# All expert-row gathers of the last stage asked for at once, into buffers that stay

## The reference, cut to what matters

```
ys = lax.map(expert_block, (xs, blk_e)).reshape(P, D)       # rows sorted by expert
out = jnp.zeros((T, D), h.dtype).at[slot_tok].add(ys * slot_w[:, None])
x = x + out
return rmsnorm(x, final_norm_g)
```

## Time and profile before

| | us |
|---|---|
| median of three runs | 2504.13 |
| the three runs | 2502.18 to 2509.46 |
| span of the profiled execution | 2504.9 |
| DVE busy in the span | 1248.2 |
| ACT busy | 1009.9 |
| POOL busy | 160.6 |

### The profile page before, as it was taken

One profiled execution on the slowest core, in us unless ns is written; L12 is line 12 of the kernel. 1 busy time (PEld: TensorE's weight loads), 2 busy tenths in 40 slices (PEclk: granted clock), 3 DMA queues, 4 the chain that ended last, 5 costly groups with the idle time before them and its releaser, 6 DMA issues. The chain is left out here.

```text
span 2504.9 us, 32948 instructions
## 1 busy us (share of the span) xinstructions
PE 2146.1 (86%) x11404; PEld 1831.7 (73%) x11405; DVE 1248.2 (50%) x1504; ACT 1009.9 (40%) x1406; POOL 160.6 (6%) x260
## 2 busy tenths in 40 slices
PE   7967999944998877999999449999999999999900
PEld 6855777734886866888888348888888888888800
DVE  3444655557011562333333455656866646656545
ACT  4543222113010453343333305645766646556421
POOL 0000000000000000000000000000000000000043
PEclk9987999967999898999999669999999999999955
DMA  3753111046343432222221335776987757757777
GB/s 110 234 207 126 51 59 43 31 165 227 124 136 131 152 118 81 74 76 79 81 75 51 146 127 203 306 271 252 386 333 278 293 217 288 302 207 298 305 277 276
DMA packets 121258, 450.54 MB, mean 180 GB/s; under 512 B 12784, under 2 KB 35824, under 8 KB 100720
## 3 DMA queue, kind: packets, MB, share of 16 engines
q1 hardware_dynamic: 76096, 296.58, 32.6%
q0 software_dynamic: 27600, 85.47, 10.1%
q10 hardware_dynamic: 17504, 67.71, 6.6%
HBM read 357.44 MB, written 92.28 MB: 180 GB/s over the span
## 5 line engine op out<-in xcount | busy, mean ns | idle before, releaser
L1795 DVE TENSOR_TENSOR expert_lo<-expert_raw,expert_hi 128x2048 fp32r<-128x2048 f32 x188 | 421.8, 2284 | 36.8 <-ACT expert_hi L1740 36.8
L1740 ACT ACTIVATE expert_hi<-expert_raw 128x2048 fp32r<-128x2048 f32 x186 | 346.0, 1912 | 17.0 <-ACT ex_y L1777 17.0
L61 PE MATMUL ex_pD<-expert_hi,ex_hT_lo 128*128 128x512 f32 x392 | 159.0, 406 | 0.0
L61 PE MATMUL ex_pG<-expert_hi,ex_xT_lo 128*128 128x512 f32 x392 | 155.9, 398 | 1.6 <-DVE ex_xT_lo L1800 1.6
L62 PE MATMUL ex_pG<-expert_lo,ex_xT_hi 128*128 128x512 f32 x392 | 155.6, 397 | 0.0
L63 PE MATMUL ex_pG<-expert_hi,ex_xT_hi 128*128 128x512 f32 x392 | 155.5, 397 | 0.0
L63 PE MATMUL ex_pD<-expert_hi,ex_hT_hi 128*128 128x512 f32 x392 | 155.3, 396 | 0.0
L62 PE MATMUL ex_pD<-expert_lo,ex_hT_hi 128*128 128x512 f32 x392 | 155.0, 395 | 0.0
L1814 DVE TENSOR_TENSOR ex_hm<-ex_sil,ex_pUa 128x256 f32<-128x256 f32 x49 | 20.6, 420 | 224.7 <-PE ex_pUa L63 223.1
L61 PE MATMUL ex_pUb<-expert_hi,ex_xT_lo 128*128 128x256 f32 x392 | 113.7, 290 | 0.0
L62 PE MATMUL ex_pUb<-expert_lo,ex_xT_hi 128*128 128x256 f32 x392 | 110.3, 281 | 0.0
(11 more groups left out here) (358 smaller groups left out, 5465.0 us busy)
## 6 DMA issues: line engine op xcount, KB each, us to landing
expert_raw<-in_w_gate SPq DMA_DIRECT2D x64, 1024.0 KB, 6.4
expert_raw<-in_w_up SPq DMA_DIRECT2D x64, 1024.0 KB, 8.9
expert_raw<-in_w_down SPq DMA_DIRECT2D x64, 1024.0 KB, 8.2
ys<-ex_y ACTq DMA_DIRECT2D x49, 512.0 KB, 8.4
z<-ff_z ACTq DMA_DIRECT2D x16, 1024.0 KB, 5.0
fb_z<-z SPq DMA_DIRECT2D x16, 1024.0 KB, 5.3
ff_xs<-in_x SPq DMA_DIRECT2D x16, 512.0 KB, 3.6
cv_xs<-in_x SPq DMA_DIRECT2D x16, 512.0 KB, 3.4
```

The source lines that it names most:

```text
L61: pe.matmul(out, lhsT=a_lo, rhs=b_hi, start=first, stop=False, skip_group_check=True)
L1740: act.activation(w_hi[:, c], raw[:, c], ACT.Copy).then_inc(s_hi, 1)
L1795: dve.tensor_tensor(w_lo[:, c], raw[:, c], w_hi[:, c], ALU.subtract).then_inc(s_lo, 1)
```

## The change

All 16 tiles get buffers of their own: `x2`, `ya` and `yb` become 128 x 16 x 1024, and every tile has its own semaphore for each of its three transfers (48 in place of 6). The sum is written over `x2`, the result over `yb`, and ACT's square over `ya`, so `acc`, `res` and `junk` are gone. POOL waits for nothing within the phase: it issues the 32 gathers one after another, with the column of `slot_of` as the index list, and `row` with its copies is gone. SP asks for the residual rows of three tiles at once, the gain behind the first, and from the fourth tile on waits for the pair sum of three tiles before (`s_y`). The order of DVE's work is add(t+1), scale(t) from the first tile on. All loops are written out.

```
-                if not is_first(t, 2):
-                    pool.wait_ge(s_acc, t - 1)
-                for k in range(2):
-                    last = pool.tensor_copy(row[:, u, k:k + 1], slot_of[:, bass.ds(t + k * NT, 1)])
-                last.then_inc(s_row, 1)
-                pool.wait_ge(s_row, t + 1)
-                pool.sem_inc(s_asked, 1)
+            for t in range(NT):
                 for k, (dst, done) in enumerate(((ya, s_a), (yb, s_b))):
-                    pool.indirect_dma_start(out=dst[:, u], out_offset=None, in_=scratch["ys"][0:NBLK * P],
+                    pool.indirect_dma_start(out=dst[:, t], out_offset=None, in_=scratch["ys"][0:NBLK * P],
                                             in_offset=bass.IndirectOffsetOnAxis(
-                                                ap=row[:, u, k:k + 1].bitcast(U32), axis=0)
-                                            ).then_inc(done[u], 16)
+                                                ap=slot_of[:, t + k * NT:t + k * NT + 1].bitcast(U32), axis=0)
+                                            ).then_inc(done[t], 16)
...
+            for t in range(NT):
+                if t >= 3:
+                    sp.wait_ge(s_y, t - 2)
+                sp.dma_start(x2[:, t], rows(scratch["x2"], t)).then_inc(s_x[t], 16)
+                if t == 0:
+                    sp.dma_start(gain[:], io["final_norm_g"]).then_inc(s_c, 16)
...
+            add(0)
             dve.wait_ge(s_c, 16)
+            for t in range(NT):
+                if t + 1 < NT:
+                    add(t + 1)
+                scale(t)
```

More of the change, by code:

```diff
@@ L1899, in combine @@
 def combine(nc, io, scratch, slot_of, out):
+    NB = 2
     ctx = ExitStack()
@@ L1906, in combine @@
         eps = sb("eps", [P, 1])
[L1907 to L1913, removed]
+        x2 = sb("x2", [P, NT, D])
+        ya, yb = sb("ya", [P, NT, D]), sb("yb", [P, NT, D])
+        ss, sd, rs = sb("ss", [P, NT]), sb("sd", [P, NT]), sb("rs", [P, NT])
         s_c, s_eps = sem("gain"), sem("eps")
[L1915 to L1918, removed]
+        s_x = [sem("x%d" % t) for t in range(NT)]
+        s_a = [sem("ya%d" % t) for t in range(NT)]
+        s_b = [sem("yb%d" % t) for t in range(NT)]
         s_y, s_acc, s_sq, s_sd, s_rs, s_r = (sem(n) for n in ("pair", "sum", "squares", "deviation", "rstd", "result"))
-        s_o = [sem("o0"), sem("o1")]
-        rows = lambda ap, t: ap.rearrange("(t p) d -> t p d", p=P)[bass.ds(t, 1)].rearrange("o p d -> (o p) d")
+        s_o = [sem("o%d" % u) for u in range(NB)]
+        rows = lambda ap, t: ap[t * P:(t + 1) * P]
         block = ctx.enter_context(nc.Block())
@@ L1925, in _ @@
         def _(sp):
-            sp.dma_start(gain[:], io["final_norm_g"]).then_inc(s_c, 16)
-            def tile(t, u):
-                if not is_first(t, 2):
-                    sp.wait_ge(s_acc, t - 1)
-                sp.dma_start(x2[:, u], rows(scratch["x2"], t)).then_inc(s_x[u], 16)
-            tiles2(sp, NT, tile)
+            for t in range(NT):
[4 more added lines that the diff above has]
+                    sp.dma_start(gain[:], io["final_norm_g"]).then_inc(s_c, 16)
         @block.gpsimd
         def _(pool):
-            def tile(t, u):
-                if not is_first(t, 2):
-                    pool.wait_ge(s_acc, t - 1)
-                for k in range(2):
-                    last = pool.tensor_copy(row[:, u, k:k + 1], slot_of[:, bass.ds(t + k * NT, 1)])
-                last.then_inc(s_row, 1)
-                pool.wait_ge(s_row, t + 1)
-                pool.sem_inc(s_asked, 1)
+            for t in range(NT):
                 for k, (dst, done) in enumerate(((ya, s_a), (yb, s_b))):
-                    pool.indirect_dma_start(out=dst[:, u], out_offset=None, in_=scratch["ys"][0:NBLK * P],
+                    pool.indirect_dma_start(out=dst[:, t], out_offset=None, in_=scratch["ys"][0:NBLK * P],
                                             in_offset=bass.IndirectOffsetOnAxis(
-                                                ap=row[:, u, k:k + 1].bitcast(U32), axis=0)
-                                            ).then_inc(done[u], 16)
-            tiles2(pool, NT, tile)
+                                                ap=slot_of[:, t + k * NT:t + k * NT + 1].bitcast(U32), axis=0)
+                                            ).then_inc(done[t], 16)
         @block.vector
@@ L1955, in _, with add, scale @@
             dve.memset(eps[:], EPS).then_inc(s_eps, 1)
[L1957 to L1962, removed]
+            def add(t):
+                dve.wait_ge(s_a[t], 16)
+                dve.wait_ge(s_b[t], 16)
+                dve.tensor_tensor(ya[:, t], ya[:, t], yb[:, t], ALU.add).then_inc(s_y, 1)
                 dve.wait_ge(s_y, t + 1)
-                dve.wait_ge(s_x[u], landed(t, u))
-                dve.tensor_tensor(acc[:, u], acc[:, u], x2[:, u], ALU.add).then_inc(s_acc, 1)
-            def scale(t, u):
+                dve.wait_ge(s_x[t], 16)
+                dve.tensor_tensor(x2[:, t], ya[:, t], x2[:, t], ALU.add).then_inc(s_acc, 1)
+            def scale(t):
                 dve.wait_ge(s_sd, t + 1)
-                dve.reciprocal(rs[:, u:u + 1], sd[:, u:u + 1]).then_inc(s_rs, 1)
+                dve.reciprocal(rs[:, t:t + 1], sd[:, t:t + 1]).then_inc(s_rs, 1)
                 dve.wait_ge(s_rs, t + 1)
[L1971 to L1976, removed]
-            dve.wait_ge(s_c, 16)
[L1978 to L1988, removed]
+                dve.scalar_tensor_tensor(yb[:, t], x2[:, t], rs[:, t:t + 1], gain[:], ALU.mult, ALU.mult).then_inc(s_r, 1)
+            add(0)
+            dve.wait_ge(s_c, 16)
+            for t in range(NT):
+                if t + 1 < NT:
+                    add(t + 1)
+                scale(t)
         @block.scalar
@@ L1992, in _, with store @@
             act.wait_ge(s_eps, 1)
-            def square(t, u):
+            def store(t):
+                act.wait_ge(s_r, t + 1)
+                act.dma_start(rows(out, t), yb[:, t]).then_inc(s_o[t % NB], 16)
+            for t in range(NT):
                 act.wait_ge(s_acc, t + 1)
-                act.activation(junk[:], acc[:, u], ACT.Square, accum_out=ss[:, u:u + 1]).then_inc(s_sq, 1)
+                act.activation(ya[:, t], x2[:, t], ACT.Square, accum_out=ss[:, t:t + 1]).then_inc(s_sq, 1)
                 act.wait_ge(s_sq, t + 1)
[L1998 to L2020, removed]
+                act.activation(sd[:, t:t + 1], ss[:, t:t + 1], ACT.Sqrt, scale=1.0 / D, bias=eps[:]).then_inc(s_sd, 1)
+                if t >= 1:
+                    store(t - 1)
+            store(NT - 1)
+            for u in range(NB):
+                act.wait_ge(s_o[u], 16 * NT // NB)
 def halves(a):
```

## The result

| | before | after |
|---|---|---|
| median of four runs, us | 2503.15 | 2474.86 |
| range of these runs | 2498.92 to 2509.46 | 2470.37 to 2476.89 |
| span of the profiled execution | 2504.9 | 2468.8 |
| its last phase | 2384.6 to 2504.9, 120.3 | 2377.0 to 2468.8, 91.8 |

The ratio of after to before is 0.988, with a 95% interval of 0.9862 to 0.9898. The forecast was 2476, the medians differ by 28.3 us (27.9 forecast). A span is not quite its execution's own time, as was said ahead of the prediction: the profiled execution after took 2470.37 us with a span of 2468.8, and in every other run the time is 1.5 to 1.6 us over the span too. The forecast carried the difference between time and span along unchanged, so it loses nothing by that.

A forecast was written before the change was run, and what follows sets the result against it. A ring of gathers waiting for sums bounds the last phase, with DMA bytes next: 2395 + 72.8 us of bytes + 9.2 us tail = 2477.0, less 0.8 for the runs' median, rounded to 2476 us; range 2468 to 2491.

The forecast's parts named there:

- The ring and the bytes under it: Last phase: gather, sum, permission, next gather takes 14.05 us per two tiles; without it bytes bound, gaining 27.9 us.
- The rate: DMA in the last phase after its first 10 us: 29.5 MB at 405 GB/s, 72.8 us.
- The rival with 353 GB/s at full share: DMA engines give no more per busy time than now; 2487 us for the runs, chance 0.25.
- The first 10 us: Start of the last phase, from 2385: 3.5 MB moved at 351 GB/s, slope left as before.
- The last landing and the tail: End of the phase: 33.0 MB moved first, last pair landed at 2467.8, then an unchanged chain of 9.2 us.
- 8 us of cover: VectorE in the last phase: sixteen tiles at 4.01 us, alone through at 2459.7, 8 us before the bytes.
- GpSimd: Issue of 32 gathers: 41 us, at most 62 us with 1.63 us each beside VectorE; no price on the path.
- The copies: GpSimd's 32 index copies, 14.9 us busy, and the waits for them go; counted within 2.35 us.
- the 2.35 us of each turn: Ring: time from the sum's end to the first gather (sequencer, copies, a wait), taken off the path.
- SP's loads: Residual loads wait for a pair sum three tiles back, not a full sum two back; some 15 us ahead.
- The rival in which gathers and loads run ahead: Stores fill the tail, bytes move without pause at 412 GB/s; 2469 us for the runs, chance 0.09.
- The slow rival: Gathers clog the engines beside stores, at 172 GB/s; end at 2528.5 us, chance 0.04.

The follow-up runs named there:

- e2: Changed kernel with only GpSimd's wait for the full sum two tiles back restored; last phase 111.6 us, median 2495.84 us.
- e3: Changed kernel with only the index copies and GpSimd's wait for them put back; last phase 91.8 us, median 2475.10 us.
- e4: Changed kernel with GpSimd's gathers waiting for the full sum four tiles back; last phase 90.8 us, median 2475.75 us.
- e7: Changed kernel with ACT issuing each tile's store seven tiles later, the last ones in threes; last phase 86.9 us, median 2467.78 us.
- e9: Changed kernel with GpSimd's wait two tiles back, index copies and old order of SP's loads put back; last phase 120.2 us, median 2502.52 us.
- e10: Changed kernel with GpSimd's gathers waiting for the full sum three tiles back; last phase 91.7 us, median 2474.40 us.
- e1: Changed kernel with GpSimd's wait for the full sum two tiles back and the index copies put back; last phase 114.6 us, median 2494.82 us.
- e6: Changed kernel without residual loads and residual sum, for measuring alone; last phase 72.1 us, median 2455.89 us.

## Why the prediction was right

*The ring and the bytes under it.* Right. The forecast phase was 2477.0 - 2384.6 = 92.4 us, measured were 91.8 and 90.9. Of the 28.5 us gained, by putting parts back one after another, 19.8 are the permission, 3.0 the copies (from nothing to 3, as e2 shows), 5.6 the order of the loads, and 0.1 all the rest. The latter parts count only while the permission is there: without it the copies cost nothing (e3). The sizes of the shares therefore depend on the order in which parts are put back.

*The rate.* I took 405 GB/s, between 403 and 412; 415 came. The stretch of 44 us in the phase before was the right guide, and the phase's own 300 GB/s was not a property of its mixture but of its gaps. The rival with 353 GB/s at full share is refuted. With it goes, for this one core, the rule of the Trainium skill, "DMA: Bandwidth & Descriptors", section Bandwidth, by which about 358 GB/s bind; 415 were measured.

*The first 10 us* moved 3.2 MB where I let 3.5 stand, but most of that is where the 10 us were laid: mine began 0.4 us into the phase. Begun 0.4 us in, the changed phase has 338 GB/s against 351, which is 0.3 us.

*The last landing and the tail.* Here terms were off and nearly cancelled, so that the phase came out within 0.6 us is in part luck. The last bytes before the tail were over 80.5 us after the phase's start (83.2 forecast), and from there to the end were 11.3 us (9.2 forecast). Of the 2.7 us before the tail some 1.7 are the rate. Another 1.3 are a miscount: I had the stores of tiles 0 to 13 moved by then, 33.0 MB in all, but ACT asks for tile 13's store only behind the square of tile 14, at 2459.54. So 62 transfers and 32.5 MB came first, and three stores stood in the tail. The start takes 0.3 back. I had the last pair's sum start at its landing; VectorE was still at the tile before for 2 us. I had given VectorE 8 us of cover over the whole phase, and on the whole it had them (a tile without a wait took it 3.79 us, 4.01 forecast), but cover over a phase is not cover at its last tile, where two pairs land close together.

*GpSimd.* 41.1 us of issue, 41 forecast; beside VectorE single gathers took up to 1.51 us (1.63 as the bound). The bound was too low: in e2 and e4 a gather took up to 1.94 us. Even 32 of those, 72 us with the 0.30 between two, would have ended before the bytes. The queue took all 32.

*The copies.* I put them within the 2.35 us of each turn. That they alone were worth at most some 3 us in the ring was missed, in the expectation of e2 and not in the forecast: the delay beside VectorE moves to the next GpSimd instruction, and what is still won there goes into a longer transfer.

*SP's loads.* I priced the new order at nothing. With the ring open that is right in effect, since bytes bound; with the ring closed it is worth 5.6 us.

*Stores in the tail.* The rival in which gathers and loads run ahead did not happen by itself, since ACT asked for each store right behind the square of the next tile. e7 brought it about, with a phase of 86.9 us where that rival's end makes 84.7.

*The slow rival.* Gathers at 172 GB/s beside stores did not come back in the changed phase after its first 10 us. The slowest 2 us there have 356 GB/s, and the slowest 4 us, under the 400 I expected of every stretch, have this row:

```profile
2395.00:2399.00 4.00, 0.00 (x0) 0.00 (x0) 3.93 (x6) 1.42 (x3) 3.08 (x4) 0.50 1.03 385
```

What made those 2 us slow before remains open. It goes with few transfers under way: in e9, with two tiles in flight, it comes again, 184 GB/s at a share of 0.81 in 2425 to 2427 and 176 at 0.83 in 2439 to 2441, nearly gathers alone. The slowest 2 us behind the first 10 are 285 GB/s in e10 and 371 in e4.

## What to carry to other kernels

Where a ring of waits and a transfer limit lie close together, price the gain by the bytes at the rate of the longest full stretch in the trace, not at the rate of the gappy stage itself. Then ask how much must be in flight to hide the way from permission to packets: here three tiles instead of two gave all of it, as far as one profile tells. Count the bytes before the last landing by the order in which each engine's program asks for them: a store behind the next tile's work may belong to the tail. Once bytes bound, the next gain lies in what the transfers leave unused at the end: here stores that waited until the loads were through won 4 to 5 us.

## What the runs showed of the hardware

One core kept 415 GB/s for 70 us with 23% of the engines' time in stores. At 2 tiles in flight (e9, e1, e2) the same work ran at 0.84 to 0.93 of the engines' time and 296 to 326 GB/s over 60 us; also the rate per busy time was lower, 350 to 360 GB/s against 400 to 403 with three tiles or more. A gather's issue takes GpSimd 0.94 us. If it starts while VectorE runs a sum or scaling of 128 x 1024 values, it ends 0.81 us after that instruction, unless its own 0.94 us end later (up to 1.97 us in all, in e6), and where GpSimd is on the path, this delay passes to whichever of its instructions is first.
